# One unread 128x512 product ahead of each attention unit's transposes, and four more ahead of the first unit

## The reference, cut to what matters

```python
for layer in range(DEPTH):                                   # DEPTH = 2
    h = rmsnorm(x, norm_mix[layer])
    z = h @ w_in[layer]
    ...
    o_a = nsa_mixer(...)       # compressed, selected and window attention, 4 heads
    o_b = diff_mixer(...)      # p[:, :, 0] - lam * p[:, :, 1]
    o_c = mlstm_mixer(...)
    o_d = dilated_mixer(...)
    x = x + jnp.concatenate([o_a, o_b, o_c, o_d], axis=-1) @ w_out[layer]
    h = rmsnorm(x, norm_ffn[layer])
    x = x + (jax.nn.silu(h @ w_gate[layer]) * (h @ w_up[layer])) @ w_down[layer]
```

## Time and profile before

| | us |
|---|---|
| median of 3 runs | 2352.38 (2352.22 to 2357.61) |
| the profiled execution, its own time | 2349.88 |
| its span, first to last instruction | 2348.1 |
| PE busy | 2157.4 (92%) |
| DVE busy | 684.4 (29%) |
| ACT busy | 322.4 (14%) |
| attention units of layer 0, first scores to last copy into `O` | 148.78 to 244.98 |
| attention units of layer 1, the same | 684.20 to 779.80 |
| mean granted TensorE clock over the span | 0.919 |

### The profile page before, as it was taken

How to read it: one execution, slowest core, us unless ns; L and a number is a source line. 1 busy time by engine, 2 the same in 40 slices (tenths; PEclk the granted TensorE clock), 3 DMA queues, 4 the chain that set the end, 5 groups by cost and what they waited for, 6 DMA issues and landing times.

```text
span 2348.1 us, 23404 instructions
## 1 busy us (share of the span) xinstructions
PE 2157.4 (92%) x9184; PEld 1265.2 (54%) x9184; DVE 684.4 (29%) x1244; ACT 322.4 (14%) x754; POOL 85.0 (4%) x124
## 2 busy tenths in 40 slices
PE   7789799997889789998989999999989799999996
PEld 3377476773467467766654444444377444444442
DVE  1335333421144334325641111111142411111113
ACT  1143100000043100001121111111010211111110
POOL 3100100000100200002000000000000000000000
PEclk9965799998965799998989999999999899999999
DMA  8310467762310367864448999999945399999995
GB/s 255 90 54 1 136 219 264 250 212 105 90 54 0 126 234 248 273 243 138 130 156 337 422 427 428 428 428 427 417 171 201 110 408 424 427 427 428 428 428 231
DMA packets 150590, 603.20 MB, mean 257 GB/s; under 512 B 16432, under 2 KB 76720, under 8 KB 123088
## 3 DMA queue, kind: packets, MB, share of 16 engines
q1 hardware_dynamic: 145536, 591.43, 64.5%
q0 software_dynamic: 4752, 10.20, 1.7%
q10 hardware_dynamic: 192, 0.05, 0.0%
HBM read 597.64 MB, written 1.10 MB: 255 GB/s over the span
## 4 chain that ended last, share of the span: by engine, by line
PE 87%; DVE 6%; ACT 2%; DMA 2%; issue 1%; DVEq 1%; SPq 0%; another core or an unknown queue 0%; ACTq 0%
PE ps L1496 27%; PE ps L613 13%; PE ps L463 7%; PE ps L619 6%; PE ps L1482 6%; PE ps L1466 5%; PE ps L1386 4%; PE ps L556 3%; PE ps L1351 2%; PE ps L596 2%; PE ps L1399 2%; PE ps L570 2%; DMA ring<-in_e_w_up 2%; PE ps L1328 1%; PE ps L585 1%
## 5 line engine op out<-in xcount | busy, mean ns | idle before, releaser
L613 PE MATMUL ps<-hT,ring 128*128 128x256 f32 x1408 | 309.9, 381 | 2.1 <-DVE hT L258 2.1
L613 PEld LDWEIGHTS ps<-hT,ring 128*128 128x128 f32 x1408 | 274.7, 196 | 33.3 <-issue 4.0
L1496 PE MATMUL ps<-ring,hT 128*64 128x512 f32 x1024 | 226.1, 594 | 4.2 <-DMA ring<-in_e_w_gate 2.6
L1496 PE MATMUL ps<-ring,qkT 128*64 128x512 f32 x1024 | 226.8, 595 | 2.9 <-ACT qkT L1656 2.9
L1496 PE MATMUL ps<-ring,late 128*64 128x512 f32 x1024 | 226.1, 594 | 2.9 <-ACT late L1643 2.9
L463 PE MATMUL ps<-ring,hT 128*128 128x494 f32 x384 | 163.0, 584 | 3.6 <-DVE hT L258 2.1
L1496 PEld LDWEIGHTS ps<-ring,hT 128*64 128x64 f32 x1024 | 72.0, 137 | 154.1 <-issue 146.5
L619 PE MATMUL ps<-ring,late 128*128 128x512 f32 x352 | 154.7, 592 | 0.0
L1496 PEld LDWEIGHTS ps<-ring,late 128*64 128x64 f32 x1024 | 72.8, 137 | 150.7 <-issue 150.7
L1496 PEld LDWEIGHTS ps<-ring,qkT 128*64 128x64 f32 x1024 | 72.5, 137 | 136.3 <-issue 134.5
L1482 PE MATMUL ps<-qkT,O 128*128 128x256 f32 x512 | 138.5, 417 | 3.4 <-DVEq L1888 3.4
(11 more groups left out here) (355 smaller groups left out, 1862.0 us busy)
## 6 DMA issues: line engine op xcount, KB each, us to landing
ring<-in_e_w_gate SPq DMA_DIRECT2D x64, 2048.0 KB, 14.8
ring<-in_e_w_down SPq DMA_DIRECT2D x64, 2048.0 KB, 13.6
ring<-in_e_w_up SPq DMA_DIRECT2D x64, 2048.0 KB, 15.8
ring<-in_ada_w SPq DMA_DIRECT2D x24, 2048.0 KB, 10.1
ring<-in_w_in SPq DMA_DIRECT2D x12, 1976.0 KB, 15.6
ring<-in_w_gate SPq DMA_DIRECT2D x22, 1024.0 KB, 7.6
ring<-in_w_up SPq DMA_DIRECT2D x22, 1024.0 KB, 9.9
ring<-in_w_down SPq DMA_DIRECT2D x22, 1024.0 KB, 11.5
```

Of the source, the lines that this page charges most:

```text
L613: last = mm(m.ps[:, c, at:at + SEQ], w[:, j, c, :], m.hT[:, j, :], start=(j == 0), stop=(j == KC - 1))
L1496: last = mm(m.ps[x * T:(x + 1) * T, out + n, :], operand[:, j, at + x * T:at + (x + 1) * T], w[x][:, j, n * 512:(n + 1) * 512], start=(j = ...
```

## The change

A function `keep_busy` computes one product of 128x512: the identity matrix is the stationary operand and half a row tile of `x` the moving one. Its result goes to PSUM bank 6 or 7 and is read by nobody. It is called four times ahead of the first unit, behind the two waits that stand there, and once in each of turns 1 to 14, between the value products and the transposes, ahead of the wait for `probs`. In turn `k` it writes the bank into which the value products of unit `k - 1` go in the next turn, so from the third unit on it first waits until DVE has read the bank for unit `k - 3` (`o_done`); before the change that same wait stood one turn later, ahead of the value products, where it still stands too.

```diff
@@ -544,8 +544,14 @@
         pe.wait_ge(s["prep_ev"], N_PREP)
         pe.wait_ge(s["gate_cols"], 1)
 
+        def keep_busy(bank):
+
+            mm(m.ps[:, bank, :], m.ident[:], m.x[:, 0, 0:512], start=True, stop=True)
+
 
         n = len(UNITS)
+        for spare in range(4):
+            keep_busy(6 + spare % 2)
         for k in range(-1, n + 2):
             if k + 1 < n:
                 kind, t, hp = UNITS[k + 1]
@@ -572,6 +578,9 @@
             if 1 <= k <= n:
                 u = k - 1
                 kind, t, hp = UNITS[u]
+                if u >= 2:
+                    pe.wait_ge(s["o_done"], u - 1)
+                keep_busy(6 + u % 2)
                 pe.wait_ge(s["probs"], u + 1)
                 if u >= 1:
                     pe.wait_ge(s["pt"], u)
```

## The result

The changed kernel takes 2339.87 us in the median (2336.61 to 2345.96), the kernel before 2352.22 in the same runs (2349.71 to 2357.61). The ratio is 0.995 with a 95% interval of 0.9933 to 0.9967, so it is faster by 0.5%, 12.4 us. The prediction was 2342.6 us, 9.8 us less than before.

What follows compares the result with a forecast made beforehand. PE's own work at 1.2 GHz was taken to bound the attention stages. With 10 of 14 units at the upper clock, +7.3 - 12.1 = -4.9 us per layer, -9.8 for two, gave 2342.6 us; range 2320 to 2367.

Steps and rivals of the forecast that it cites:

- What bounds the stages: In the two attention stages, PE's own work at 1.2 GHz was said to bound, 70.4 us of the stage's 96.2.
- The clock reacts to full rows without a pause: On PE, the clock was said to rise after stretches of full 128-row products without a pause, 4.0 us in L596.
- Price of a product: On PE, a 128x512 float32 product was put at 0.86 us with the clock up and 1.71 us at 0.50.
- The four: The products ahead of each layer's first unit delay the stage by 5.4 us, or 6.9 if the clock does not react.
- The fourteen, clock low: Products in a layer's turns at the lower clock: 23.9 us, 18.5 after what waits hide, 25.4 with the four ahead.
- n = 10 of 14 units: In each attention stage, 10 of 14 units were expected to run with the clock up, giving -4.9 us per layer.
- The clock up all through: An attention stage with every unit at the upper clock was put at 79.2 us, 17.0 less, with DVE's 48 us counted.
- The sum: A layer changes by 25.4 x (14 - n)/14 - 17.0 x n/14; n = 10 gives -4.9 us, -9.8 for two.
- The added wait: The wait for `o_done` of two units back, ahead of each product in the turns, was costed at nothing.
- What the profile would show: In both stages: clock about 0.85, length near 91 us, L576 about 2 us in most units, new L594 waits for DVE.
- the draw: Rival for the stages: clock up in only 8 or 9 units, +2.3 to -3.7 us, 2349 to 2355 us, chance 0.33.
- The products change nothing: Rival for the stages: the clock ignores the products, both layers pay 25.4 us, +51, 2403 us, chance 0.05.

Runs made afterwards that it cites:

- few_rows: The changed kernel with all 18 added products of a layer cut to 32 of 128 rows, same 512 columns; 2415.73 us, ratio 1.0259 to the kernel before.
- turns_only: The changed kernel without the four products ahead of the first unit, the fourteen in the turns kept; 2350.11 us, ratio 0.9984 to the kernel before.
- four_only: The changed kernel with only the four products ahead of the first unit, none in the turns; 2363.77 us, ratio 1.0048 to the kernel before.
- half_columns: The changed kernel with the fourteen products of the turns cut to 128x256, the four ahead still 128x512; 2364.92 us, ratio 1.0055 to the kernel before.

## Why the prediction was right, and where not

- **What bounds the stages.** Right: PE at 1.2 GHz. few_rows shows it from the other side: 18 products without the clock make a stage 31 us longer.
- **The clock reacts to full rows without a pause.** Right as to the rows, and shown by few_rows. "Without a pause" is not shown apart: at 169.81 us the clock stayed up through a wait of 2.6 us, and at 217.0 it fell with no wait ahead of it.
- **Price of a product.** 0.86 and 1.71 us were predicted, 0.91 and 1.82 measured in the queue, from the start of one to the start of what follows.
- **The four.** 5.4 us predicted, 6.2 measured. The clock rose 5.2 us behind their start, not 4.0 as in the row of L596. The prediction counted on them only to make the first units warm; turns_only shows that they are worth more than they cost.
- **The fourteen, clock low.** With the four 25.4 us a layer predicted; few_rows gives 31, and some 28 for full rows. Too small by some 3 us, of which 18 x 0.11 = 2.0 by the price above; this is the term that was most off.
- **n = 10 of 14 units.** Right. Behind the four the first stage is at 0.50 for the four rows above, 30.7 us with their edges, and at 1.00 for 52.7. At few_rows' 8.6 us a unit the 30.7 us hold 3.6 units, so 10.4 had the clock up, at 5.1 us each. In the second stage the same working gives 34.1 us, 4.0 units, and 10.0 at 5.3 us. These are estimates. The mean clock of 0.80 must not be read as 8.4 units (0.5 + 0.5 x 8.4/14): it is a mean over time, and a unit at the upper clock takes less time. In the first stage the clock fell four times: at 172.6 and 206.7 us behind the two `mlstm` waits, at 196.5 behind the new wait of 2.1 us for the softmax of `dil` 1 (L594 for L876), and at 217.0, from where it stayed down for 13.6 us, the tail that the prediction names.
- **The clock up all through.** -17.0 us predicted, a stage of 79.2. Fourteen units at 5.1 or 5.3 us and the four products make 77 and 80 us, an estimate, so the size was right. The reason given for it was not: I put DVE's 48 us in the place of PE's 35.2 + 12.0 = 47.2, since the transposes would wait for the softmax. PE's waits stayed at 9.7 us, with one new one of 2.1 for DVE where several were expected. PE's queue went on to bind, with the products at their full price. With 47.2 the same sum gives 78.4, so it was luck that the wrong engine had nearly the same length.
- **The sum.** -4.9 us a layer predicted, -6.6 and -2.6 measured in the profiled run, -9.2 against -9.8 for both. The remaining 3 us of the median's 12.4 are outside the stages; they are within the interval of the ratio (7.8 to 15.8 us) and within what the unchanged parts vary by.
- **The added wait.** Right: no wait of L549 on `o_done` stands among PE's waits.
- **What the profile would show.** The clock in the stages was 0.80, not 0.85, and the mean stage 91.3 us, as forecast (91). Of the signs of being wrong none came: the clock is above 0.75, L549 waits for no `o_done`, and the time past the stages moved by 2.3 us, which is within its scatter.
- **The rivals.** The forecast was closest, by its time and by its number of units. Its 10 units and the draw's 8 or 9 lie close together, though, and the estimate of n is no finer than a unit. "The products change nothing" is refuted for full rows and is exactly what happens with 32 rows.

## What to carry to other kernels

A product that nobody reads can pay for itself where PE's own small products run at 1.2 GHz: look first whether the stage's granted clock is low while PE is busy, and give the product all 128 rows. Count it at its full price in the queue, for a packed queue hides little, and look for waits first: three in each of two waits a layer gained about as much again as the 18 of the change. Here the burst at the start was worth more than it cost, but only with products behind it in the turns: alone it made the kernel slower (four_only). Do not read a mean clock as a share of the work: work at the upper clock takes less of the time.

## What the runs showed that I had not expected

- With 32 of 128 rows the same products leave the clock at 0.50 for 127 us, though PE is busy for 122 of them.
- Without the burst at the start, the same product in each turn had the clock up only after 43 and 50 us (turns_only), with it the stage's clock was 0.80. Why it came back sooner after a fall in the changed kernel is open.
- A product of half the columns in each turn was no better than none: half_columns is 25 us slower than the change, 12.2 us slower than the kernel before, and as slow as four_only.
- The unchanged part ahead of the second layer's first products takes up to 3.6 us more in one kernel than in another, with a longer stretch at the lower clock (20.3 against 13.4 us in the rows above).
